# Two-layer hybrid backbone step (convolution, state space and attention branches): state copies, query/key norm and B's scaling placed anew

## What is computed

```python
h = _rmsnorm(x, norm_g) * (1.0 + scale) + shift
z = h @ w_in          # conv_in, conv_gate, ssm_in, ssm_gate, q, k, v, attn_gate, merge
ya = _conformer_conv(conv_in, ...)             # GLU, depthwise conv of 31 taps, LayerNorm, SiLU
yb = _s5_bidirectional(ssm_in, ...)            # state recurrence both ways, 32 groups x 64 states
    # lam_bar = exp(lam * dt);  b_bar = ((lam_bar - 1.0) / lam)[..., None] * (b_re + i b_im)
yb = yg_a * sigmoid(yg_b)                      # of gelu(yb) @ w_ssm_glu
q = _rmsnorm(q per head, q_norm_g);  k = _rmsnorm(k per head, k_norm_g)
q, k = rotary(q), rotary(k)                    # latent tokens only; they also read a cached k, v
s = (q . k) * HEAD_DIM ** -0.5;  p = softmax(s);  o = p v
br_x = (branch_x * silu(gate_x)) @ w_x_out     # x = A (conv), B (ssm), C (attention)
x = x + gate * ((g_a*br_a + g_b*br_b + g_c*br_c) @ w_out)
```

## Time and profile before

| what | before |
|---|---|
| median of 3 runs (lowest, highest) | 713.28 us (711.75, 714.95) |
| the profiled execution, its own time | 713.04 us |
| its span in the trace | 711.0 us |
| mean granted clock of PE | 0.969 of full |
| PE busy | 652.4 us, 92% of the span |
| PEld busy | 466.5 us, 66% |
| DVE busy | 551.5 us, 78% |
| ACT busy | 297.3 us, 42% |
| POOL busy | 36.4 us, 5% |
| moved by DMA | 117.65 MB, 165 GB/s mean |

### The profile page before, as it was taken

The page is one execution under the profiler, slowest core; times in us unless marked ns, Lnnn a source line. Parts: engine busy times, 40 slices in busy tenths (PEclk is TensorE's granted clock), DMA queues, the critical chain, the costliest instruction groups (busy, mean ns, idle before and its releaser), DMA issues. The chain is left out here.

```text
span 711.0 us, 9584 instructions
## 1 busy us (share of the span) xinstructions
PE 652.4 (92%) x3573; PEld 466.5 (66%) x3573; DVE 551.5 (78%) x1024; ACT 297.3 (42%) x454; POOL 36.4 (5%) x49
## 2 busy tenths in 40 slices
PE   3689899996997999998999899999897999999997
PEld 1368674553843688877887687465664578877885
DVE  3679689989777886589975657998878698887663
ACT  2564350212533445435455736011445444436441
POOL 2100001111000000010001010012000000010000
PEclk9989889998998999999999999999998999999999
DMA  8992817654383274654543437660632346655631
GB/s 289 348 275 70 275 36 232 239 183 141 123 272 122 75 229 146 179 176 149 167 158 95 138 136 252 205 240 11 198 112 66 89 121 184 199 165 164 201 104 59
DMA packets 67305, 117.65 MB, mean 165 GB/s; under 512 B 11052, under 2 KB 15484, under 8 KB 67260
## 3 DMA queue, kind: packets, MB, share of 16 engines
q1 hardware_dynamic: 66980, 116.94, 51.9%
q10 hardware_dynamic: 280, 0.11, 0.1%
HBM read 112.51 MB, written 1.38 MB: 160 GB/s over the span
## 5 line engine op out<-in xcount | busy, mean ns | idle before, releaser
L805 PE MATMUL proj<-raw,hT 128*128 128x512 f32 (+1 forms) x320 | 132.0, 558 | 0.0
L1584 DVE SCALAR_TENSOR_TENSOR cvacc<-cvpad,taps,cvacc 128x256 f32<-128x256 f32 x240 | 98.6, 477 | 0.3
L805 PEld LDWEIGHTS proj<-raw,hT 128*128 128x128 f32 x320 | 58.2, 190 | 58.8 <-issue 57.0
L1477 DVE TENSOR_TENSOR raw_split<-raw,wide_split 128x1024 fp32r<-128x1024 f32 x56 | 67.9, 1220 | 21.6 <-ACT wide_split L1193 20.9
L1193 ACT ACTIVATE wide_split<-raw 128x1024 fp32r<-128x1024 f32 x56 | 58.6, 1059 | 55.9 <-PE proj L835 55.9
L834 PE MATMUL proj<-raw_split,H_split 128*128 128x512 f32 x192 | 75.4, 393 | 0.0
L833 PE MATMUL proj<-wide_split,H_split 128*128 128x512 f32 x144 | 57.9, 402 | 4.7 <-DVE raw_split L1477 4.7
L835 PE MATMUL proj<-wide_split,H_split 128*128 128x512 f32 x144 | 56.9, 395 | 0.0
L1477 DVE TENSOR_TENSOR raw_split<-raw,utok_split 128x1024 fp32r<-128x1024 f32 x28 | 34.2, 1220 | 15.1 <-ACT utok_split L1193 15.1
L1193 ACT ACTIVATE utok_split<-raw 128x1024 fp32r<-128x1024 f32 x28 | 29.6, 1058 | 34.8 <-PE proj L835 34.8
L834 PEld LDWEIGHTS proj<-raw_split,H_split 128*128 128x128 f32 x192 | 36.4, 190 | 7.3
(11 more groups left out here) (252 smaller groups left out, 1327.0 us busy)
## 6 DMA issues: line engine op xcount, KB each, us to landing
raw<-in_w_in SPq DMA_DIRECT2D x104, 512.0 KB, 4.3
raw<-in_w_ada SPq DMA_DIRECT2D x48, 512.0 KB, 5.3
raw<-in_w_out SPq DMA_DIRECT2D x16, 512.0 KB, 3.8
raw<-in_w_ssm_glu SPq DMA_DIRECT2D x8, 512.0 KB, 7.0
raw<-in_w_ssm_out SPq DMA_DIRECT2D x8, 512.0 KB, 4.3
raw<-in_w_attn_out SPq DMA_DIRECT2D x8, 512.0 KB, 3.7
...
```

Of the source, the lines that this page charges most:

```text
L805: m = T.matmul(proj.bank((l, u, s))[:, 0:n], lhs[:, s, kt, :], w[:, i, :], start=(kt == 0), stop=last)
L1477: return V.tensor_tensor(out, a, b, op)
L1584: m = V.scalar_tensor_tensor(acc, src, taps[:, t, j:j + 1], acc, ALU.mult, ALU.add)
```

## The change

1. A new stage "HY" directly behind the scan copies the states of parts 0 and 1 of Y (ACT and DVE), where before they came behind the query/key norm and the taps that follow it. The scan's place in the list moves ahead of "ag".
2. Two new stages "sumsq" on ACT behind K 0: ten 128x64 squares with an accumulated sum for each stream, in place of DVE's square and reduction.
3. The root of q's sum of squares is no longer multiplied into q: it goes into the scale of the exponential (with the 1/8), and into the negated maximum. DVE's part of "qkn" is then q's gain, and the rotary for latent q.
4. k's norm, gain and rotary go to GpSimd (`k_norm`), with a semaphore of its own, and start behind the scan.
5. B's scaling goes from DVE to GpSimd; in layer 0 it stands behind `pre`, no longer between cp and the scan.
6. PE claims the long bank ahead of its first product with v (p = 2), not at the block's head.
7. The two sums for the GELU are made at p = 2 and 3 of the first attention block, one each, and not both at 3.
8. The taps are placed anew; in layer 0 the stage "taps" goes behind "preE", and the first high/low split of "cg" ahead of the last hT.

```diff
-TAPS_IN_ZONE = (16, 8)
-TAPS_IN_ATT = (((8, 8, 8, 8, 8), (7, 4, 4, 7, 0)), ((6, 6, 6, 6, 6), (7, 4, 4, 7, 0)))
+TAPS_IN_ZONE = (26, 14)
+TAPS_IN_Y = (8, 5, 6)
+TAPS_IN_ATT = (((8, 8, 4, 4, 2), (4, 4, 4, 4, 0)), ((6, 6, 3, 3, 2), (4, 4, 4, 4, 0)))
+CONV_B = (12, 18)
...
-             ("chunks", "ca", 4), ("pre", 0, 1), ("unit", "ca"), ("taps", 0), ("preE", 0, 0), ("pack",), ("preE", 0, 1)]
+             ("chunks", "ca", 4), ("pre", 0, 1), ("unit", "ca"), ("preE", 0, 0), ("pack",), ("preE", 0, 1), ("taps", 0),
+             ("bbar", 0)]
...
-            + [("UT",), ("S",), ("cp",)] + turn + [("bz", 0), ("convT", 0), ("convT", 1), ("unit", "q"), ("unit", "kv"),
-               ("adaE", l, 2), ("K", 0), ("unit", "sg"), ("bz", 1), ("K", 1), ("unit", "ag")] + nxt("adaE", n, 0)
-            + [("scan", 0, NCHUNK), ("qkn",), ("conv", TAPS_IN_ZONE[l], None), ("Y",), ("adaT", l, 2)] + nxt("adaT", n, 0)
+            + [("UT",), ("S",), ("cp",), ("bz", 0), ("convT", 0), ("convT", 1), ("unit", "q"), ("unit", "kv"), ("adaE", l, 2),
+               ("K", 0), ("sumsq", 0), ("sumsq", 1), ("unit", "sg"), ("bz", 1), ("K", 1), ("scan", 0, NCHUNK), ("HY",),
+               ("unit", "ag")] + nxt("adaE", n, 0)
+            + [("qkn",), ("conv", TAPS_IN_ZONE[l], None), ("Y",), ("adaT", l, 2)] + nxt("adaT", n, 0)
...
-                            ("ada", 0, 1, 0, DT), ("adaE", 0, 1), ("adaT", 0, 1), ("hT", 1, 0), ("hT", 1, 1),
-                            ("early", 1, 0), ("chunks", "cg", 1), ("early", 1, 1))]
+                            ("ada", 0, 1, 0, DT), ("adaE", 0, 1), ("adaT", 0, 1), ("chunks", "cg", 1), ("hT", 1, 0),
+                            ("hT", 1, 1), ("early", 1, 0), ("early", 1, 1))]
...
-                    long_.claim(pe, ("pv", l, s))
...
+                        if p == 2:
+                            long_.claim(pe, ("pv", l, s))
...
+                elif k == "sumsq":
+                    s = stg[1]
+                    proj.drained(act, (l, "q", s))
+                    proj.drained(act, (l, "kv", s))
+                    for i in range(HEADS + KV):
+                        h = i // 2 + 4 * (i % 2) if i < HEADS else i
+                        m = S.activation(sq_out[:, s, HD * i:HD * i + HD], qk[:, s, HD * i:HD * i + HD], ACT.Square,
+                                         accum_out=qst[:, s, 0, h:h + 1])
+                    m.then_inc(qk_sq, 1)
...
-                                             bias=nmx[:, s, h, 0:1], scale=HD ** -0.5, accum_out=nmx[:, s, h, 1:2])
+                                             bias=nmx[:, s, h, 0:1], scale=qst[:, s, 2, h:h + 1],
+                                             accum_out=nmx[:, s, h, 1:2])
...
+                elif k == "HY":
+                    dve.wait_ge(scan_done, l + 1)
+                    for q in range(2):
+                        states_bwd(q)
...
-                        if s == 0 and p == 3:
-                            for s_ in range(NS):
-                                gelu_sum(l, s_)
+                        if s == 0 and p in (2, 3):
+                            gelu_sum(l, p - 2)
...
+            def k_norm(l, s):
+
+                pool.wait_ge(qk_sq, ls(l, s))
+                sums, tmp, rs = (qst[:, s, i, :] for i in range(3))
+                Q.tensor_scalar(tmp[:, 0:HEADS], sums[:, 0:HEADS], 1.0, HD * EPS, ALU.mult, ALU.add)
+                link(Q.tensor_scalar(tmp[:, HEADS:], sums[:, HEADS:], 1.0 / HD, EPS, ALU.mult, ALU.add))
+                tt_(rs, tmp, st[:, 128:128 + HEADS + KV], ALU.pow).then_inc(qk_rs, 1)
...
+                link(tt_(k3, k3, rs[:, HEADS:].unsqueeze(2).to_broadcast([P, KV, HD])))
+                m = tt_(k3, k3, qkg[:, 1:2, :].to_broadcast([P, KV, HD]))
...
+                elif k == "bbar":
+                    pool.wait_ge(pre_done, 2 * (l + 1))
+                    pool.wait_ge(tab_done, 1)
+                    if l:
+                        side.filled(pool, ("K", l - 1, 7))
...
```

More of the change, by code:

```diff
@@ L1173, in half_tanh, with states_fwd @@
                     S.activation(th_view(key), proj.bank(key)[:, :], ACT.Tanh, scale=0.5).then_inc(proj.freed(key), 1)
+            def states_fwd(q):
+                S.activation(HY[0:64, q % 2].rearrange("p g r s k -> p (g r s) k"),
+                             H[0:64, 0:NCHUNK, 32 * q:32 * q + 32].rearrange("p k x -> p x k"),
+                             ACT.Copy).then_inc(hy_fwd, 1)
             highs = [0]
@@ L1549, in qk_norm @@
                 if s == 0:
                     m.then_inc(qk_done, 1)
-                else:
-                    link(m)
-                    dve.wait_ge(rope_in, 16)
-                    link(tt_(qkt[:, :].rearrange("p (h d) -> p h d", d=HD), q3,
-                             rope[:, 0:1, :].to_broadcast([P, HEADS + KV, HD])))
-                    r5 = prob[:, :, :].rearrange("p a b -> p (a b)")[:, 0:QK]
-                    for a in range(2):
-                        five = lambda t: t.rearrange("p (h f a c) -> p a h f c", f=2, a=2, c=16)
-                        sin = rope[:, 1, :].rearrange("p (o f a c) -> p a o f c", o=1, f=2, a=2)[:, a]
-                        link(tt_(five(r5)[:, a], five(qk[:, s, :])[:, 1 - a],
-                                 sin.to_broadcast([P, HEADS + KV, 2, 16])))
-                    tt_(qk[:, s, :], qkt[:, :], r5, ALU.add).then_inc(qk_done, 1)
@@ L1563, in qk_norm @@
-                dve.wait_ge(qk_done, ls(l, s))
+                    return
+                link(m)
+                dve.wait_ge(rope_in, 16)
+                tt_(qkt[:, 0:W].rearrange("p (h d) -> p h d", d=HD), q3, rope[:, 0:1, :].to_broadcast([P, HEADS, HD]))
+                for a in range(2):
+                    five = lambda t: t.rearrange("p (h f a c) -> p a h f c", f=2, a=2, c=16)
+                    sin = rope[:, 1, :].rearrange("p (o f a c) -> p a o f c", o=1, f=2, a=2)[:, a]
+                    m = tt_(five(q_turn)[:, a], five(qk[:, s, 0:W])[:, 1 - a], sin.to_broadcast([P, HEADS, 2, 16]))
@@ L1901, in _ @@
                 elif k == "Y":
[L1902 to L1912 removed]
+                    for q in range(2, 5):
+                        for _ in range(TAPS_IN_Y[q - 2]):
+                            conv_tap(*taps_left.pop(0))
+                        if q < 4:
+                            side.filled(dve, ("Y", l, q - 2))
+                            states_bwd(q)
                 elif k == "cback":
@@ L2006, in rsqrt_mean @@
                 tt_(dst, tmp, st[:, 128:128 + count], ALU.pow).then_inc(done, 1)
+            def k_norm(l, s):
[4 more added lines that the diff above has]
+                tt_(rs, tmp, st[:, 128:128 + HEADS + KV], ALU.pow).then_inc(qk_rs, 1)
+                pool.wait_ge(qk_rs, ls(l, s))
+                pool.wait_ge(rows_in, 80 * (l + 1))
+                proj.drained(pool, (l, "kv", s))
+                k = qk[:, s, HEADS * HD:QK]
+                k3 = k.rearrange("p (h d) -> p h d", d=HD)
+                link(tt_(k3, k3, rs[:, HEADS:].unsqueeze(2).to_broadcast([P, KV, HD])))
+                m = tt_(k3, k3, qkg[:, 1:2, :].to_broadcast([P, KV, HD]))
+                if s == 0:
+                    m.then_inc(k_done, 1)
+                    return
+                link(m)
+                pool.wait_ge(rope_in, 16)
+                tt_(k_tmp[:, 0, :].rearrange("p (h d) -> p h d", d=HD), k3, rope[:, 0:1, :].to_broadcast([P, KV, HD]))
+                for a in range(2):
+                    five = lambda t: t.rearrange("p (h f a c) -> p a h f c", f=2, a=2, c=16)
+                    sin = rope[:, 1, :].rearrange("p (o f a c) -> p a o f c", o=1, f=2, a=2)[:, a]
+                    m = tt_(five(k_tmp[:, 1, :])[:, a], five(k)[:, 1 - a], sin.to_broadcast([P, KV, 2, 16]))
+                link(m)
+                tt_(k, k_tmp[:, 0, :], k_tmp[:, 1, :], ALU.add).then_inc(k_done, 1)
             Q.memset(cond[:, :, :], 0.0).then_inc(zeroed, 1)
@@ L2024, in _ @@
                 elif k == "qkn":
+                    pool.wait_ge(scan_done, l + 1)
                     for s in range(NS):
-                        pool.wait_ge(qk_sq, ls(l, s))
-                        rsqrt_mean(qst[:, s, 2, :], qst[:, s, 0, :], HD, HEADS + KV, qst[:, s, 1, :], qk_rs)
+                        k_norm(l, s)
+                elif k == "bbar":
[3 more added lines that the diff above has]
+                        side.filled(pool, ("K", l - 1, 7))
+                    for i in range(2):
+                        side.drained(pool, ("bT", l, i))
+                    co = [coef[:, j, G * l:G * l + G].unsqueeze(2).to_broadcast([P, G, GC]) for j in range(2)]
+                    t0, t1 = (bzf[:, W * i:W * i + W].rearrange("p (g c) -> p g c", g=G) for i in range(2))
+                    b0, b1 = (bbar[:, r, :, :] for r in range(2))
+                    tt_(t0, b0, co[1])
+                    link(tt_(t1, b1, co[1]))
+                    tt_(b0, b0, co[0])
+                    link(tt_(b1, b1, co[0]))
+                    tt_(b0, b0, t1, ALU.subtract)
```

(1 more changed line is left out.)

88 lines of the change are left out of this document (33 added, 55 removed).

## The result

| what | before | after |
|---|---|---|
| median of 4 runs (lowest, highest) | 713.51 us (711.75, 714.95) | 691.31 us (689.65, 693.59) |
| profiled execution, its own time | 713.04 us | 691.89 us |
| span in the trace | 711.0 us | 690.1 us |
| mean granted clock of PE | 0.969 | 0.989 |

The ratio is 0.9697, with a 95% interval of 0.9662 to 0.9732: 3.0% faster, 22 us. The forecast of 692.0 us and its range of 685 to 704 hold the result.

The account below looks back on a forecast made before the run. TensorE (PE), busy 92% of the span, was taken as the bound. Terms 3.7 + 5.3 + 5.9 + 2.4 + 5.9 − 1.5 − 0.5 = 21.2 us off 713.04 gave 691.8, rounded 692.0 us; range 685 to 704.

Parts of the forecast that it names:

- (b): First Y, layer 0: HY copies directly behind the scan shorten PE's pause by 3.2 us; clock staying up adds 2.1.
- (f): B's scaling on GpSimd: six operations in layer 1 slow DVE beside them, 1.5 us lost (0 to 4).
- (h): Taps moved from the attention to the zone and combinations, where DVE has other work: 0.5 us lost (0 to 2).
- (a): First stages of layer 0: earlier cg split about 1.3 us, moved stage taps 2.0 plus 0.4; 3.7 us gained.
- second rival: Clock falls at Y anyway and GpSimd blocks DVE in full in layer 1: 697.7 us, up to 702; chance 0.17.
- (c): First attention, layer 0: block 1's first scores no longer wait for the drain, clock included; 5.9 us gained.
- (e): Second-layer attention: as in layer 0, pauses of 1.71 and 1.87 us go, plus clock; 5.9 us gained.
- (d): Second-layer Y: the pause shrinks by 1.0 us until the matrix is next, the clock adds 1.4; 2.4 us gained.
- (g): k's norm on GpSimd, 14 operations a layer: some 10 us, hidden before the first scores; priced 0.
- slower rival: Port contention: GpSimd's k norm blocks DVE before Y, 25 us a layer lost, 742 us; chance 0.04.

Follow-up runs that it names:

- run 9: The changed kernel with layer 0's stage taps back ahead of preE, the earlier first split of cg kept: 694.88 us, ratio 0.9731.
- run 2: The changed kernel with the first two state copies put back behind the norm and the taps: 691.00 us, ratio 0.9681.
- 6: The changed kernel with layer 1's scaling of B on GpSimd held back until the chunk sums S are made: 690.60 us, ratio 0.9681.
- run 4: The changed kernel with the long bank's claim back at the head of the block: 690.75 us, ratio 0.9681.
- 1: The kernel before with only the scan and state copies moved ahead of ag (stage HY): 706.61 us, ratio 0.9918.
- 12: The changed kernel measured again, with nothing altered: 690.83 us, ratio 0.9682.
- run 10: The changed kernel with 10 taps instead of 26 behind q's norm in layer 0, 16 more at C0: 694.42 us, ratio 0.9729.
- 7: The changed kernel with M's DMAs on two queues and layer 1's B scaling held back until S is made: 690.39 us, ratio 0.9667.
- run 8: The kernel before with the changed attention taps and GELU sums, the long bank's claim where it was: 703.50 us, ratio 0.9851.
- run 3: The kernel before with the later claim of the long bank alone: 707.73 us, ratio 0.9909.

## Why the prediction was right, and where not

- **What bounds it, and the sum.** Right: 21.2 us forecast for the profiled execution, 21.15 found (20.85 of it inside the span). That the two agree so closely is luck: (b) came out 1.7 lower and (f) and (h) 1.5 better, and the same kernel's second profile is 2.3 us shorter. The next wait was named and sized: M, at 2.2 us, in both layers (2.23, 1.60).
- **(a)** 3.7 against 3.14 in the profile, but by another split: "about 1.3" for the earlier split of cg is nothing that run 9 shows, and the stage taps, at 1.99 + 0.4, measured 4.0.
- **(b)** The 3.2 was right. Its cause as written, "Now HY is done directly behind the scan", is only one of two: run 2 takes it back and the time stays. The scan's end was written as 151.1; it is 146.68, mainly since the 3.1 us by which S comes earlier were left out there. The failed step is the clock: "2.2 is nearest to the first, so I take it". The pauses' lengths do not decide it. The rows of before already spoke against it: the clock was at 0.50 behind the 2.67 at 218.80, and it also fell behind the 1.99 at 82.18, a window that the forecast did not read:

```profile
82.20:86.70 4.50, 3.73 (x22) 3.28 (x23) 0.00 (x0) 3.83 (x6) 0.00 (x0) 0.64 1.04 404
```

 In the runs, eight pauses before Y of layer 0 and four others have this clock over the 4.5 us behind them:

| run | pause, us | clock |
|---|---|---|
| 9 | 2.08 | 0.62 |
| 6 | 2.12 | 0.62 |
| after | 2.23 | 0.62 |
| 4 | 2.27 | 1.00 |
| 1 | 2.32 | 1.00 |
| 12 | 2.40 | 0.66 |
| 10 | 2.51 | 0.62 |
| 2 | 2.80 | 0.65 |
| 2, layer 1 | 2.73 | 1.00 |
| 4, layer 1 | 1.72 | 1.00 |
| after, layer 1 | 1.60 | 1.00 |
| 7, layer 1, inside Y | 1.86 | 0.64 |

 A pause of 2.73 kept 1.00 and one of 1.86 did not. The 2.1 should have stood as a bound, not as the value. The second rival had this part, and it came true alone.
- **(c) and (e)** 5.9 each against 6.12 and 5.89. The size was read from the pauses and the clock behind them, and that holds whatever removes them. The cause given, that the scores "no longer wait for the drain", holds only for the kernel before: with fewer taps and one sum at the block's end the drain is there in time (run 4), and that lighter load alone gives 10.6 us (run 8), the claim alone 6.5 (run 3).
- **(d)** 2.4 against 2.63, 1.40 from the pause and 1.23 from the clock.
- **(f)** 1.5 against 1.0, by two errors that offset each other. "Six are 3.7 us" was short: one operation takes 1.04 us undisturbed (the sum had 0.61), and in layer 1 the six take 8.7 (384.52 to 393.21). And "half" was not what reached PE: DVE's operations from 384.59 to 398.53 are 4.7 us longer in all than undisturbed, and all but 1.0 of it is hidden. The Trainium skill, GPSIMD Engine Reference, section "Engine selection", has 2-input elementwise work about twice as slow on GpSimd; here it is 1.04 against 0.69, 1.5 times.
- **(g)** Priced 0, and it costs 0, but "some 10 us" was 21.7. The slower rival had the contention the wrong way round: DVE's taps were not held in the changed kernel, and one multiply on GpSimd was. The Trainium skill, SBUF — State Buffer, section "Who interferes with whom", has the one that comes second fully blocked until the other's instruction is through. The rows agree in part. DVE's split of 2.32 is about its own 1.22 and one GpSimd operation of 1.04. But the held multiply did not get in between two instructions of the train, and in run 2 GpSimd's 0.52 beside taps of 0.63 and 0.67 is far less loss than a full block on either side.
- **(h)** −0.5 against +0.47 (0.55 and −0.08). That is half a microsecond outside its bounds of 0 to −2, less than two profiles of the same kernel differ by. That taps can cost at the combinations is right all the same: run 10 shows 16 more at C0 costing 3.6.

Not settled: what decides whether the clock falls behind a pause of some 2 us; how the 4.0 us of run 9 divide; why one multiply on GpSimd waits for the end of the taps when other operations there don't; and what the norm's move (2 to 4) and B's scaling in layer 0 (5) are worth alone, which no run takes back.
